# Moving work around the joints between the six sites of a two-block transformer kernel

## What is computed

```python
def second_block(x, norm_gains, w_ffn_gate, w_ffn_up, w_ffn_down, w_in, w_out, diff_lambda, diff_subln_gain):
    for layer in range(DEPTH):
        g = norm_gains[layer]
        h = rmsnorm(x, g[0])
        x = x + 0.5 * rmsnorm(swiglu(h, w_ffn_gate[layer, 0], w_ffn_up[layer, 0], w_ffn_down[layer, 0]), g[1])
        h = rmsnorm(x, g[2])
        x = x + rmsnorm(token_mixer(h, w_in[layer], w_out[layer], diff_lambda[layer], diff_subln_gain[layer], layer), g[3])
        h = rmsnorm(x, g[4])
        x = x + 0.5 * rmsnorm(swiglu(h, w_ffn_gate[layer, 1], w_ffn_up[layer, 1], w_ffn_down[layer, 1]), g[5])
    return x
```

## Time and profile before

| What | us |
|---|---|
| Median of 3 runs | 1435.7 |
| Lowest and highest of them | 1433.32, 1436.69 |
| The profiled execution: its own time | 1436.06 |
| Its span, first to last instruction | 1434.1 |
| PE busy | 1398.1 |
| DVE busy | 1018.7 |
| ACT busy | 726.7 |
| POOL busy | 86.7 |

### The profile page before, as it was taken

The page is one execution under the profiler, slowest core; times in us unless marked ns, Lnnn a source line. Parts: engine busy times, 40 slices in busy tenths (PEclk is TensorE's granted clock), DMA queues, the critical chain, the costliest instruction groups (busy, mean ns, idle before and its releaser), DMA issues.

```text
span 1434.1 us, 22170 instructions
## 1 busy us (share of the span) xinstructions
PE 1398.1 (97%) x8053; PEld 1159.8 (81%) x8053; DVE 1018.7 (71%) x1693; ACT 726.7 (51%) x1244; POOL 86.7 (6%) x103
## 2 busy tenths in 40 slices
PE   5999999999999999999999999999999999999998
PEld 2778747869768888888888888888888888888887
DVE  2588454469677777787686777877777876877776
ACT  3433264345565444475664444654445756644444
POOL 0301211220110000000200000000000002000000
PEclk9999999999999999999999999999999999999999
DMA  9622184275235655754345556646655643455662
GB/s 354 195 88 89 59 285 175 88 221 150 88 133 170 198 189 175 248 176 146 118 133 176 175 193 193 211 153 202 197 183 177 195 142 118 133 176 178 202 196 98
DMA packets 185654, 243.03 MB, mean 169 GB/s; under 512 B 4560, under 2 KB 154608, under 8 KB 185456
## 3 DMA queue, kind: packets, MB, share of 16 engines
q1 hardware_dynamic: 182272, 229.43, 49.9%
q0 software_dynamic: 2736, 10.55, 2.2%
q10 hardware_dynamic: 576, 2.10, 0.4%
HBM read 241.01 MB, written 1.05 MB: 169 GB/s over the span
## 4 chain that ended last, share of the span: by engine, by line
PE 69%; DVE 12%; DMA 9%; ACT 5%; issue 4%; POOL 0%; SPq 0%; DVEq 0%; ACTq 0%; POOLq 0%
PE bank L1977 33%; PE bank L2496 13%; PE bank L2498 7%; DMA weight_ring<-in_w_ffn_up 5%; DVE weights_low L1573 3%; ACT weights_high L992 3%; DVE arena L1567 2%; PE bank L2104 2%; DMA weight_ring<-in_w_ada 2%; DMA weight_ring<-in_w_ffn_down 2%; PE bank L1958 1%; DMA weight_ring<-in_w_in 1%; PE bank L2324 1%; PE bank L2474 1%; PE bank L2475 1%
## 5 line engine op out<-in xcount | busy, mean ns | idle before, releaser
L1573 DVE TENSOR_TENSOR weights_low<-weight_ring,weights_high 128x1024 fp32r<-128x1024 f32 x328 | 393.3, 1223 | 128.8 <-ACT weights_high L992 128.7
L992 ACT ACTIVATE weights_high<-weight_ring 128x1024 fp32r<-128x1024 f32 x328 | 334.6, 1048 | 102.1 <-PE bank L1977 62.0
L2496 PE MATMUL bank<-input_split,weights_high 128*128 128x512 f32 x1280 | 319.5, 391 | 0.0
L2496 PEld LDWEIGHTS bank<-input_split,weights_high 128*128 128x128 f32 x1280 | 234.7, 188 | 45.0
L2498 PEld LDWEIGHTS bank<-input_split,weights_low 128*128 128x128 f32 x1280 | 174.6, 190 | 12.5
L2498 PE MATMUL bank<-input_split,weights_low 128*128 128x256 f32 x1280 | 178.5, 282 | 0.0
L1977 PE MATMUL bank<-weights_high,hidden_high 128*128 128x512 f32 x352 | 138.8, 394 | 1.2 <-DVE hidden_low L1682 1.2
L1066 ACT ACTIVATE silu_gate<-gate_sum 128x256 f32<-128x256 f32 x88 | 36.7, 418 | 202.0 <-DVE gate_sum L1660 200.5
L1977 PE MATMUL bank<-weights_low,hidden_high 128*128 128x512 f32 x352 | 137.9, 392 | 0.0
L1977 PE MATMUL bank<-weights_high,hidden_low 128*128 128x512 f32 x352 | 137.0, 389 | 0.0
L1977 PE MATMUL bank<-input_split,weights_high 128*128 128x256 f32 x576 | 105.6, 285 | 0.0
(11 more groups left out here) (358 smaller groups left out, 2267.5 us busy)
## 6 DMA issues: line engine op xcount, KB each, us to landing
weight_ring<-in_w_ffn_gate SPq DMA_DIRECT2D x44, 1024.0 KB, 5.3
weight_ring<-in_w_ffn_up SPq DMA_DIRECT2D x44, 1024.0 KB, 5.3
weight_ring<-in_w_ffn_down SPq DMA_DIRECT2D x44, 1024.0 KB, 4.9
weight_ring<-in_w_in SPq DMA_DIRECT2D x32, 1024.0 KB, 5.3
weight_ring<-in_w_ada SPq DMA_DIRECT2D x24, 1024.0 KB, 6.0
weight_ring<-in_w_out SPq DMA_DIRECT2D x16, 1024.0 KB, 5.0
weight_ring<-in_w_in SPq DMA_DIRECT2D x24, 512.0 KB, 4.8
gain_row<-in_norm_gains POOLq DMA_DIRECT2D x6, 512.0 KB, 4.1
```

The lines of the kernel that those rows point to most:

```text
L992: A(unit_in(WH, U), unit_source(U), ACT.Copy).then_inc(s_high, 1)
L1573: TTn(unit_in(WL, U), unit_source(U), unit_in(WH, U).bitcast(F32), ALU.subtract).then_inc(s_low, 1)
L2496: mm(b[:, :].rearrange("p (h n) -> p h n", h=2), unit_in(WH, U)[:, k, :], HX[:, k, :, :], start=(k == 0), stop=False, skip_group_check=True)
```

## The change

1. **Down units.** PE runs tile 0 of units a+4 and a+5 (half 0, half 1), then tile 0 of a+6, then tile 1 half by half through all three. The splits of a+5 and a+6 come earlier, ahead of the last hidden chunk's rounding.
2. **Units 2 and 3 of the next site** (after an ffn). ScalarE's copies move into the tail, one after each tile's root. GpSimd makes unit 2's low part (`third_low`); VectorE hands it on with a copy of one element after its eight `input_ready`.
3. **Square sums.** After an ffn the first of the four sums is taken by ScalarE inside the tail, the second by VectorE (`tensor_tensor_reduce`, 512 columns, ahead of tile 1's reciprocal), the third after the fourth `input_high`, the fourth last. After a mix the first stands where it was, the third after the fourth `input_high`, the others last.
4. **Update of tile 1** (not at the last site): half 0 in two quarters, ahead of `gained(1, 1)`.
5. **Turns.** PE transposes chunks 0 to 3 of tile 0, a half warm-up, chunks 0 to 3 of tile 1, begins `first_units`, and transposes chunks 4 to 7 of both tiles inside it, after its third chunk.
6. **Norm sum.** In an ffn it stands after five matmuls of the next unit instead of three; in a mix after block 0's product instead of before it.
7. **First splits of the later ffn sites:** ScalarE's units 4 and 5 and VectorE's low parts of 4 and 5 move behind steps of the first hidden chunk.

```diff
+                if i < 5 and kind == "ffn":
+                    third = unit_base[i + 1] + EARLY - 2
+                    pool.wait_ge(s_high, turn[third] + 1)
+                    pool.tensor_tensor(unit_in(WL, third), unit_source(third), unit_in(WH, third).bitcast(F32), ALU.subtract).then_inc(*done("third_low", i + 1))
...
+                after_ffn = i and SITES[i - 1][0] == "ffn"
+                if i and not after_ffn:
                     x_square(i, 0, 0)
-                    x_square(i, 0, 1)
-                if i and SITES[i - 1][0] == "ffn":
-                    high(unit_base[i] + EARLY - 1)
                 for c in range(KD):
+                    if i and c == 4:
+                        x_square(i, 1, 0)
...
+                            if t and i < 5 and SITES[i][0] == "ffn":
+                                x_square(i + 1, 0, 0)
...
+                    if i < 5 and SITES[i][0] == "ffn":
+                        high(unit_base[i + 1] + EARLY - 2 + t)
...
                 high(a + 5)
+                high(a + 6)
                 hidden_high(1, f + 2, None, to=2)
-                high(a + 6)
-                for U in ahead[1:]:
+                for U in ahead[1:2]:
                     high(U)
...
                 for U in ahead[:1]:
                     low(U)
+                low(a + 5)
                 dve.wait_ge(s_used, a + 4)
                 dve.wait_ge(s_silu, f + 2)
                 TTn(hbuf[:, 1, :], B[3][:, 0:T], sgate[:, 1, :], ALU.mult).then_inc(s_h, 1)
-                low(a + 5)
+                low(a + 6)
                 hidden_low(1, f + 2, to=2)
-                low(a + 6)
-                for U in ahead[1:]:
+                for U in ahead[1:2]:
                     low(U)
...
+                if i and SITES[i - 1][0] == "ffn":
+                    dve.wait_ge(*at("third_low", i))
+                    CP(stat[:, 61:62], eps[:, 0:1]).then_inc(s_low, 1)
...
+                gained(0, 0)
+                gained(0, 1)
+                scale(0)
+                update(0, 0, slice(0, 512))
+                update(0, 1, slice(512, 1024))
+                gained(1, 0)
...
+                    if SITES[i][0] == "ffn":
+                        dve.wait_ge(*at("x_new", i, 0, 1))
+                        dve.tensor_tensor_reduce(out=XN2[:, 0, 512:1024], in0=X[:, 0, 512:1024], in1=X[:, 0, 512:1024], scale=1.0, scalar=0.0, op0=ALU.mult, op1=ALU.add, accum_out=stat[:, 1:2]).then_inc(*done("x_mean", "first tile", i + 1))
+                    scale(1)
+                    update(1, 0, slice(0, 256), "first")
+                    update(1, 0, slice(256, 512))
+                    gained(1, 1)
+                update(1, 1, slice(512, 1024))
...
                 turned(0, (0, 1, 2, 3))
+                if i:
+                    warm(1, 256)
+                    turned(1, (0, 1, 2, 3))
+                    return lambda: (turned(0, (4, 6)), turned(1, (4, 6)), turned(0, (5, 7)), turned(1, (5, 7)))
...
+                    if c == 2:
+                        rest_turned()
...
-                    if site is not None and k == 3:
+                    if site is not None and k == 5:
                         norm_sum(site)
...
-                down(1, a + 4, f, False)
...
+                lasts = ((1, a + 4, f), (0, a + 5, f + 1), (2, a + 6, f + 2))
+                for rest in (lasts[:2], lasts[2:]):
                     for hf in range(2):
-                        for par in range(2):
...
+                        for par, U, ready in rest:
+                            pe.wait_ge(s_hl, ready)
+                            pe.wait_ge(s_low, turn[U] + 1)
+                            down_row(par, U, 0, False, U == a + 6, (hf,))
...
-                first_units(i, u0, [B[PB2[key]] for key in firsts], 0)
+                first_units(i, u0, [B[PB2[key]] for key in firsts], 0, rest_turned)
+                products(2, 3)
                 norm_sum(i)
-                products(2, 4)
+                products(3, 4)
```

More of the change, by code:

```diff
@@ L1614, in inverse @@
                     for hf in range(2):
-                        dve.wait_ge(*at("sum_squares", "site", i, t, hf))
+                        if (t, hf) == (0, 1) and i and SITES[i - 1][0] == "ffn":
+                            dve.wait_ge(*at("x_mean", "first tile", i))
+                        else:
+                            dve.wait_ge(*at("sum_squares", "site", i, t, hf))
                 TTn(stat[:, 6:8], stat[:, 0:4:2], stat[:, 1:4:2], ALU.add).then_inc(*done("x_mean", "sum", i))
@@ L2435, in site_norm, with warm @@
             def site_norm(i):
-                def warm(count):
+                def warm(count, width=512):
                     for _ in range(count):
-                        mm(B[0][:, :], ident, KB[:, 0:512], start=True, stop=True)
+                        mm(B[0][:, 0:width], ident, KB[:, 0:width], start=True, stop=True)
                 def turned(t, chunks):
@@ L2445, in turned @@
                                 pe.wait_ge(*at(*r))
[L2446 removed]
+                        if i == 0:
+                            pe.wait_ge(*at("final_scaled", t, c // 4))
+                        elif t and c < 2:
+                            pe.wait_ge(*at("x_new", i - 1, 1, 0, "first"))
+                        else:
+                            pe.wait_ge(*at("x_new", i - 1, t, c // 4))
                         last = tr(B[X_BANK[c]][:, half * T + t * P:half * T + (t + 1) * P], X[:, t, c * P:(c + 1) * P], ident)
@@ L2760, in _ @@
             for i, (kind, n) in enumerate(SITES):
-                site_norm(i)
-                (ffn if kind == "ffn" else mix)(i, n)
+                (ffn if kind == "ffn" else mix)(i, n, site_norm(i))
 INPUTS = ["x", "c", "ctx", "c_ctx", "w_ada", "w_in", "w_uq", "w_ukv", "w_pw", "w_fourier", "sgu_ln_g", "sgu_ln_b", "w_s", "b_s",
```

91 lines of the change are left out of this document (50 added, 41 removed).

## The result

The changed kernel took 1444.79 us (median of 5 runs, 1441.25 to 1447.82) against 1434.85 us for the kernel before beside it (1433.32 to 1436.69): a ratio of 1.0068 with a 95% interval of 1.0051 to 1.0086. It is 9.9 us slower, where 2.1 us were forecast, and it lies above the range given. The profiled execution of the changed kernel has 1447.82 us of its own and a span of 1446.0; against the profiled one of before (1436.06, span 1434.1) that is +11.9.

The account below looks back on a forecast made before the run. PE was taken as the bound, busy 1398.1 of 1434.1 us. First joint -0.2, third +0.2, fourth +2.1 and the rest 0 made +2.1, from a median of 1435.7 to 1437.8 us; range 1432.2 to 1441.5.

Parts of the forecast that it names:

- DMAs: Ring loads at the third joint: gate load released later, up unit's low part at 947 against 948.7 wanted; cost nothing.
- Contention: Tail of the three ffn joints: GpSimd's split delays VectorE's square sum, 0.8 us of PE each, bounds 0 and 2.2.
- The norm sum in a mix: Later norm sum delays VectorE's evictions: PE stands 1.1 us at first scores, plus 0.8 or 0.9 later, in each mix.
- The rival without a stall: In the mixes VectorE has missed slack and both stalls go at both joints: -1.8, 1433.9 us; chance 0.13.
- The first joint's stretch: Last down matmul to `first_units`: 6.10 us becomes 3.4 plus 0.88, so -1.82; bounds -2.7 and -1.
- Third and fourth joints: Last down matmul to `first_units`: 0.64 us earlier, but eight transposes return as 0.88; net +0.24 at the third.
- without the contention: Rival at the tail: GpSimd slips through, 0.8 us saved at three joints, third joint -0.58; total -0.3, 1435.4; chance 0.14.
- Second and fifth: Joints after a mix: quarter ready 0.9 us earlier, 0.88 us of transposes moved behind it; 0, bounds -0.5 and +0.5 each.
- Part 7: Reordered splits beside PE's 5.5 us of `gate_up`, some 0.6 us to spare: 0, up to 0.5 if cover goes.
- The slower rival: Half-clock stretches if gaps behind the half warm-up exceed about 1.5 us; three joints at 1.7, +5.1, 1442.9; chance 0.13.

Follow-up runs that it names:

- hand_over_early: The changed kernel with VectorE's hand-over copy of unit 2's low part ahead of its input splits instead of behind them; 1445.14 us, ratio 1.0072.
- third_unit_before_tail: The changed kernel without GpSimd's split and the hand-over: ScalarE and VectorE split unit 2 ahead of the tail, as before; 1440.4 us, ratio 1.0045.
- norm_in_mix_back: The changed kernel with the norm sum of a mix back ahead of block 0's product; 1444.95 us, ratio 1.0068.
- the hybrid: The changed kernel with norm sums and first splits as before, GpSimd's split only ahead of a mix and behind the last update; 1434.01 us, ratio 0.9994.
- the first four experiments: The changed kernel with one edit each: norm_in_mix_back, gpsimd_after_update, hand_over_early and third_unit_before_tail; 1444.95, 1442.1, 1445.14 and 1440.4 us.
- gpsimd_after_update: The changed kernel with GpSimd's split of unit 2 also waiting for the last update of the residual; 1442.1 us, ratio 1.0051.
- warm_up_of_after_filled: The changed kernel with two warm-up products of 512 columns in place of the half one ahead of tile 1's turns; 1446.78 us, ratio 1.0082.

## Why the prediction was wrong

Its direction of each part was mostly right; the forecast failed on sizes, and on one term that was put at nothing.

- **DMAs: "nothing".** The step that failed most. Two loads in flight, the up load later for it, ScalarE's split of it late: all of that was seen, and even put at 14.3 us behind the start of `first_units` (945 against 930.7), where it was 13.3. The step asked only for the first reader of that unit, and PE indeed did not wait for it. What was left out is the rest of ScalarE's and VectorE's queues: 3.5 us late, they did not catch up over the next pair, and PE's wait came there, 2.00 us at 974.83, for a hidden low part. "If 2 us more were lost there, PE would wait" was measured on the wrong reader. Measured: 2.8 us (hand_over_early) to 3.0 us (third_unit_before_tail) between profiled executions, the 1.7 us of the half clock behind the wait included. Where the clock stayed full (norm_in_mix_back) the same late loads left ffn2 at +1.52, 0.7 to 0.9 us above these two.
- **Contention: 0.8 a joint.** Measured 1.34. The mechanism was right, its order not: GpSimd did not "wait out the two updates", it got in between them, so the update of tile 0 paid and not the square sum. Three joints, 1.6 us more than forecast. The Trainium skill's rule ("SBUF — State Buffer", "Who interferes with whom") that the one that starts first keeps the port agrees with the 2883 ns of the second update beside the 2.47 us of GpSimd's split; what the rule leaves the reader to see is that the gap between two queued instructions is a place to get in.
- **The norm sum in a mix.** Right. Together with the wait that went it was put at +1.6 and +1.9, measured +1.71 and +1.54, with 0.99 us at the first scores against 1.1 forecast. The rival without a stall is refuted. Taken back alone it gives 1.25 and 1.02 us: the other half microsecond of a mix comes back as a longer wait ahead of the norm sum, which the prediction did not have.
- **The first joint's stretch: -1.8.** Measured -0.89 in the kernel after and -2.24 once the contention is away; of the 0.93 between it and the forecast 0.54 are that contention again, which had been counted in with 0.8, and the rest is that the joint wins 0.38 less even without it (-2.24 where -2.62 was worked out). The source named, the 1.97 us for unit 2's load, is right: with it alone removed from the kernel before, J1 is at -2.19.
- **Third and fourth joints: +0.2 each.** Measured +1.17 and +1.13, without the contention -0.17 and -0.19 (forecast for that case: -0.58 each). **Second and fifth: 0.** Measured +0.27 each, inside the bounds.
- **Part 7: "0, up to 0.5 if that cover goes".** The cover went: 0.54, 0.23 and 0.53 us in three sites, one execution each. The sum had the 0.
- **The clock.** The slower rival had the right mechanism and half of the place. Of the nine waits of 1.44 us at joints (three each in after, norm_in_mix_back and hand_over_early) four were followed by 3.4 us at half clock and five were not; the length and the 1.7 us lost are as forecast, the boundary of "about 1.5" is not a sharp one. The surest place was the wait inside a gate-and-up site. By the medians' clock (0.9974 in the mean of after's five runs, 0.9987 in the 26 of before beside the second set of experiments) it accounts for up to 0.0013 x 1443 = 1.9 us of the 9.9, the half clock counted with the ring among them.

Against the forecast of +2.1: +2.9 for the ring with its half clock, +1.6 for the contention, +1.3 for part 7, +0.5 for J2 and J5, +1.2 because the three joints are worth less even without the contention (-2.24, -0.17 and -0.19 where -2.62, -0.58 and -0.58 were worked out), -0.3 for the mixes. That makes 9.3 of the 10.3 us that the columns of the profiled execution add up to; the medians are 9.9 apart. The rest is not taken apart: bodies of the gate-and-up sites stay at +0.05 to +0.55 even in the hybrid, and joints run at half clock in some of the executions. Nor is it shown why the three joints win less than worked out. These prices rest on differences between single profiled executions; of the first four experiments only gpsimd_after_update (2.7 us) and third_unit_before_tail (4.4 us) show their gain in the medians as well. Why an execution with a wait of 1.44 us keeps its clock and the next does not stays open. The wait for unit 2's load at the first joint differs by 3 us between kernels and executions (1.20 to 4.46 us); that was seen and not pursued.

## What to carry to other kernels

When a copy that frees a buffer is moved, follow the engines that its load feeds over more than their next step: here one tiny copy, placed behind eight input splits, let two loads go out within 1 us of each other, and the two engines that split them came to a wait of TensorE one pair later; that cost up to 3.0 us, beside the 4.0 us of the contention at three joints. An operation given to an idle GpSimd must be placed against VectorE's critical instructions, not only after its data: behind the last update the same split held nothing up, and amid the updates it cost some 1.34 us at each of three joints. And before a joint is rebuilt in seven parts, try the one part that the longest wait in it points to: one split moved away from a late load gave 2.2 us, more than any other kernel tried here, and the other parts together gave nothing.

## What the runs showed of the hardware

- A GpSimd operation of 1024 columns that became ready during a VectorE update took effect between that update and the next one queued behind it: the second lasted 2883 ns instead of some 620, while GpSimd's took 2.47 us instead of the 2.39 behind the last update (after against gpsimd_after_update).
- A wait of PE of 1.83 to 2.08 us inside a gate-and-up site was followed by 3.4 us at half clock in all four profiled executions where it occurred (after, gpsimd_after_update, norm_in_mix_back, warm_up_of_after_filled), and waits of 0.59 to 1.50 us there by none. At the joints waits of 1.44 us were followed by such a stretch in four of nine cases. Ahead of the first site a wait of 2.06 to 2.07 us was in all thirteen profiled executions, and the clock fell to half there in seven of them. So the length of a wait alone did not decide. A stretch of 3.4 us costs 1.7; in the fourth site the wait and what came behind it made 3 us together.
